# Two edits in a two-block kernel: the transposes of masked weights left out, and rotary partners moved by DMA instead of by products

## The reference

```
k_prev = jnp.concatenate([jnp.zeros_like(kb[:, :1]), kb[:, :-1]], axis=1)
kk = jnp.concatenate([k_prev, kb], axis=2)
s = jnp.einsum('bnqkgd,bnjkd->bnkgqj', qb, kk) * (HEAD_DIM ** -0.5)
mask = band[None] & ((kj >= ATTN_BLOCK)[None] | has_prev[:, None, None])
```

```
q = (rms_norm(cq, q_a_norm) @ w_qb).reshape(b, s, MLA_HEADS, MLA_QK)
q_rope = rope(q[..., MLA_NOPE:], positions)      # x1*cos - x2*sin, x1*sin + x2*cos
kv = (rms_norm(ckv, kv_a_norm) @ w_kvb).reshape(b, s, MLA_HEADS, MLA_NOPE + MLA_DV)
```

## Time and profile before

| | |
|---|---|
| device time, median of three runs | 1911.07 us |
| runs | 1910.46, 1911.07, 1912.54 us |
| span of the profiled execution (first to last instruction) | 1909.2 us |
| mean granted TensorE clock | 0.974 |
| TensorE busy | 1858.1 us (97%) |
| VectorE, ScalarE, GpSimd busy | 869.7, 774.6, 875.8 us |
| DMA, mean over the span | 91 GB/s |

### The profile page before, as it was taken

How to read it: one execution, slowest core, us unless ns; L and a number is a source line. 1 busy time by engine, 2 the same in 40 slices (tenths; PEclk the granted TensorE clock), 3 DMA queues, 4 the chain that set the end, 5 groups by cost and what they waited for, 6 DMA issues and landing times.

```text
span 1909.2 us, 25178 instructions
## 1 busy us (share of the span) xinstructions
PE 1858.1 (97%) x8910; PEld 1520.7 (80%) x8910; DVE 869.7 (46%) x1287; ACT 774.6 (41%) x1242; POOL 875.8 (46%) x1176
## 2 busy tenths in 40 slices
PE   5899999999999999999999999999999999999997
PEld 4898888888888777888888888788888878787776
DVE  8983232121126797532121126841355551466653
ACT  8753343232224477433232334423333342334662
POOL 1025455554556521655455545664445445372222
PEclk8589999999999999999999999999999999999998
DMA  4234333333323321333332333352232233231111
GB/s 162 68 99 152 96 93 104 90 99 97 101 88 99 97 72 27 111 89 99 96 102 89 99 98 90 99 150 89 88 87 79 78 89 89 62 119 56 36 53 44
DMA packets 51428, 173.59 MB, mean 91 GB/s; under 512 B 6688, under 2 KB 7072, under 8 KB 50704
## 3 DMA queue, kind: packets, MB, share of 16 engines
q1 hardware_dynamic: 49968, 169.72, 30.1%
q10 hardware_dynamic: 1376, 2.72, 0.5%
HBM read 161.21 MB, written 2.10 MB: 86 GB/s over the span
## 4 chain that ended last, share of the span: by engine, by line
PE 37%; issue 29%; POOL 27%; DVE 5%; ACT 1%; POOLq 0%; DMA 0%; ACTq 0%; SPq 0%; DVEq 0%
POOL wlo L501 27%; PE ps L997 10%; PE ps L999 10%; PE ps L998 10%; PE ps L1474 1%; PE ps L1465 1%; PE ps L1464 1%; PE ps L1220 1%; PE ps L1187 1%; DVE E L338 0%; DVE bt L334 0%; PE ps L1149 0%; DVE E L333 0%; PE ps L1399 0%; PE ps L1402 0%
## 5 line engine op out<-in xcount | busy, mean ns | idle before, releaser
L501 POOL TENSOR_TENSOR wlo<-raw,whi 128x256 fp32r<-128x256 f32 x1152 | 863.1, 781 | 984.7 <-ACT whi L548 876.1
L548 ACT ACTIVATE whi<-raw 128x1024 fp32r<-128x1024 f32 x288 | 302.0, 1052 | 369.7 <-PE ps L999 362.9
L997 PE MATMUL ps<-Ch,whi 128*128 128x512 f32 x912 | 362.7, 398 | 0.6 <-POOL wlo L501 0.6
L999 PE MATMUL ps<-Ch,wlo 128*128 128x512 f32 x912 | 355.8, 390 | 0.0
L998 PE MATMUL ps<-Cl,whi 128*128 128x512 f32 x912 | 355.5, 390 | 0.0
L997 PE MATMUL ps<-Ah,whi 128*128 128x512 f32 x640 | 255.0, 398 | 1.7 <-DVE Al L1693 1.6
L997 PE MATMUL ps<-Bh,whi 128*128 128x512 f32 x640 | 250.4, 391 | 0.0
L999 PE MATMUL ps<-Ah,wlo 128*128 128x512 f32 x640 | 249.6, 390 | 0.0
L998 PE MATMUL ps<-Al,whi 128*128 128x512 f32 x640 | 249.3, 390 | 0.0
L999 PE MATMUL ps<-Bh,wlo 128*128 128x512 f32 x640 | 249.2, 389 | 0.0
L998 PE MATMUL ps<-Bl,whi 128*128 128x512 f32 x640 | 249.1, 389 | 0.0
(11 more groups left out here) (374 smaller groups left out, 2134.9 us busy)
## 6 DMA issues: line engine op xcount, KB each, us to landing
raw<-in_w SPq DMA_DIRECT2D x288, 512.0 KB, 3.6
u<-in_xch SPq DMA_DIRECT2D x1, 2048.0 KB, 8.3
swap<-vsb SPq DMA_DIRECT2D x16, 128.0 KB, 2.3
swap<-zz SPq DMA_DIRECT2D x16, 128.0 KB, 2.3
h<-in_xfm SPq DMA_DIRECT2D x2, 1024.0 KB, 7.1
out<-h SPq DMA_DIRECT2D x8, 256.0 KB, 2.0
bB<-in_bc SPq DMA_DIRECT2D x1, 1024.0 KB, 10.3
bC<-in_bc SPq DMA_DIRECT2D x1, 1024.0 KB, 12.8
```

The costliest lines, as they stand in the source:

```text
L501: last = nc.gpsimd.tensor_tensor(wlo[:, r, cc], raw[:, r, cc], whi[:, r, cc].bitcast(F32), ALU.subtract)
L548: nc.scalar.activation(whi[:, slot, :], raw[:, slot, :], ACT.Copy).then_inc(hi_ready, 1)
L997: nc.tensor.matmul(out, whi[:, slot, w], xh, start=first, stop=False)
L999: return nc.tensor.matmul(out, wlo[:, slot, w], xh, start=False, stop=last)
```

## The change

In the grouped-query attention the transposes of an even pair start at k = 1 (PE), so that the block of weights that query block 0 has for its missing predecessor is not transposed: three instead of four for each of the two units. ACT copies only the 384 columns that were written there.

In the latent attention the four `partners` products behind the kvb strips are gone. SP moves the partners instead: `query_swap(l)` copies four pieces of 32 partitions (64 KB each) of `qr[:, l]` into `acc` (even l) or `std` (odd l), which are free by then. DVE waits for these copies (`query_in`) where it waited for the product, and reads the partner from SBUF. SP's copies stand in its order behind the loads of strips 276 (l = 0 and 1), 277 (l = 2) and 278 (l = 3), so the loop over strips is written out from 276 to 279.

```diff
+            def query_swap(l):
+
+                sp.wait_ge(evac, OUT0["kvb"] + 1)
+                if l >= 2:
+                    sp.wait_ge(rope_done, 19 + l - 1)
+                for b in (0, 64):
+                    for lo, hi in ((b, b + 32), (b + 32, b)):
+                        sp.dma_start(query_part[l % 2][lo:lo + 32, :], qr[hi:hi + 32, l, :]).then_inc(query_in[l % 2], 16)
...
+                elif t == S0["kvb"] + 1:
+                    query_swap(0)
+                    query_swap(1)
+                elif t in (S0["kvb"] + 2, S0["kvb"] + 3):
+                    query_swap(t - S0["kvb"])
...
-                    nc.scalar.copy(pt1[:, un % 2, :], ps[:, 2 + un % 2, :]).then_inc(pt_ready, 1)
+                    kept = slice(P if pair % 2 == 0 else 0, TOK)
+                    nc.scalar.copy(pt1[:, un % 2, kept], ps[:, 2 + un % 2, kept]).then_inc(pt_ready, 1)
...
-                    for k in range(4):
+                    for k in range(1 - pair % 2, 4):
                         last = nc.tensor.transpose(ps[:, 2 + un % 2, k * P:(k + 1) * P], sm1[:, un % SLOTS1, k // 2, k % 2 * P:(k % 2 + 1) * P], C("ident"))
...
                 short_strip("kvb", l, 4, 2, "L", XT["lat"], 3)
-                pe.wait_ge(evac, OUT0["kvb"])
-                if l >= 2:
-                    pe.wait_ge(rope_done, 18 + l)
-                partners(qr[:, l, :], SX + l % 2)
...
-                rotate_by(4 + l, qr[:, l, :], qr[:, l, :], ps[:, SX + l % 2, :], rcos[:, :], rsin[:, :], ev[:, 0, :], ev[:, 1, :])
+                V.tensor_tensor(ev[:, 0, :], qr[:, l, :], rcos[:, :], ALU.mult)
+                dve.wait_ge(query_in[l % 2], 64 * (l // 2 + 1))
+                ch.link(V.tensor_tensor(ev[:, 1, :], query_part[l % 2][:, :], rsin[:, :], ALU.mult))
+                V.tensor_tensor(qr[:, l, :], ev[:, 0, :], ev[:, 1, :], ALU.add).then_inc(rope_done, 1)
```

More of the change, by code:

```diff
@@ L264, in program @@
         part_in = [sem("part_in0"), sem("part_in1")]
+        query_in = [sem("query_in0"), sem("query_in1")]
         vt_ps = sem("vt_ps")
@@ L310, in program @@
         squares = (sq, cy)
+        query_part = (acc, std)
         def over(x, axis, n):
@@ L471, in _ @@
             single_strips(E0, E1)
-            with sp.Fori(E1, NS // RING) as i:
+            V0, V1 = (S0["kvb"] + 1 + LAG) // RING, (S0["kvb"] + 3 + LAG) // RING + 1
+            with sp.Fori(E1, V0) as i:
+                for r in range(RING):
+                    next_strip(i, r)
+            single_strips(V0, V1)
+            with sp.Fori(V1, NS // RING) as i:
                 for r in range(RING):
@@ L1728, in rotate_first @@
                 V.tensor_tensor(dst, part_bank, s1, ALU.add).then_inc(rope_done, 1)
[L1730 to L1734, removed]
             def feature_lows(pair):
```

## The result

The changed kernel takes 1915.46 us (median of nine runs, 1914.28 to 1917.84), against 1911.33 us for the kernel before beside it (nine runs, 1910.02 to 1912.54). The ratio is 1.0023, with a 95% interval of 1.0014 to 1.0033. So it is slower, by 4.1 us of the medians; 3.9 were predicted. The profiled execution has a span of 1912.7 us against 1909.2, 3.5 us more.

What follows compares the result with a forecast made beforehand. TensorE, busy 97% of the span, was taken to bound the kernel. Kvb's +5.4 us (pause and half clock, products gone) less 1.5 us for transposes gave 1911.07 + 3.9 = 1915.0 us; own range 1912 to 1918, 8 in 10 1909.5 to 1918.5.

Steps and rivals of the forecast that it cites:

- The transposes: Phase q: sixteen transposes left out at 0.11 us each, 1.76 us, of which 1.5 come through; bounds 0.4 and 2.0.
- The rival in which VectorE holds phase q: Phase q: TensorE's earlier arrival turns into waiting, only 0.4 us gained; +5.0 us in all, 1916.1; 15%.
- The four products: Phase kvb: four partner products gone from TensorE at 0.90 us each, 3.6 us saved if nothing replaces them.
- When the copies land: Phase kvb: first copies, issued behind strip 276's load from 1723.45, land at 1728.6; bounds 1727.7 and 1729.4.
- The rival with 4.3: Phase kvb: copies land 4.3 us after first issue, at 1727.4 to 1727.7; about 1.0 us less, 1914.0; 9%.
- What waits behind it: Phase kvb: key row 4 leaves PSUM at 1730.8, so TensorE stands still 7.0 us before the third strip.
- The rival "in time": Phase kvb: copies land before TensorE feels them, both savings stand; 5.1 us faster, 1906.0; 8%.
- The clock: Phase kvb, after TensorE's pause: half clock for some 4 us of products, losing 1.9 us; bounds 0 and 3.2.
- The rival "the clock stays up": Phase kvb: no half clock after TensorE's pause; 1.9 us less, 1913.1; 6%.
- The last copies: Scores after kvb: VectorE comes 0.8 to 1.1 us late, 1.38 us idle time absorbs it; counted as nothing.
- The rival that priced it at 1.1 us: Scores after kvb: VectorE's 1.1 us lateness isn't absorbed; +5.0 us in all, 1916.1; 12%.
- The total: Whole kernel: 5.4 - 1.5 = +3.9 us; span 1913.1 from 1909.2, median 1915.0 from 1911.07.

Runs made afterwards that it cites:

- The sixth experiment: Changed kernel with VectorE's rotation 0 put behind the second kvb strip's key rows, 1 and 2 behind the third's, 3 behind the fourth's; 1908.61 us, ratio 0.9986.
- the third: Changed kernel with each query tile's partners copied as soon as the tile is out of PSUM, into places of their own; 1906.90 us, ratio 0.9977.
- the seventh experiment: Changed kernel with the copies for l = 3 issued right behind those for l = 2, behind the load of strip 277; 1916.27 us, ratio 1.0026.
- the fourth kernel: Changed kernel with the copies of the first two query tiles moved one load forward, behind that of strip 275; 1910.25 us, ratio 0.9998.

## Why the prediction was right, step by step

The predicted 1915.0 us stands against 1915.46, and the mechanism is the one predicted. One term, the last copies, was wrong, and one argument, on the clock, rests on a misread row.

- *The transposes.* Predicted 1.76, of which 1.5 come through; measured 1.64. The step that held some back for VectorE was not needed: two pairs take 11.53 us, from 11.74, so VectorE kept up, and the wait before the last rotated query grew by 0.08 us only. The rival in which VectorE holds phase q is out.
- *The four products.* Predicted 0.90 each and 3.6 in all; measured 3.56.
- *When the copies land.* GpSimd's part was to be 0.5 us quicker; it is 3.23 instead of 3.68. The load was to follow within 0.5 us; it is 0.03. The landing was put 5.15 us behind the first copy, and is 5.46 (1721.21 to 1726.67), within the bounds. The rival with 4.3 is out. By the estimate that the prediction works out from the Trainium skill ("DMA: Bandwidth & Descriptors", section "Anatomy of one DMA — SWDGE (gpsimd) path"), which gives figures for another path, it would have been 3.95; measured on this queue, behind a 512 KB load, it is 1.5 us more.
- *What waits behind it.* Predicted a pause of 7.0 us, measured 7.3, which is the landing's difference. The sixth experiment shows that it is carried by key row 4, the third that it goes when the copies come early. The rival "in time" needed a landing 7.0 us earlier than predicted for both savings, and 3.9 us earlier to be faster than before at all; it came 0.3 us later behind the strip's end.
- *The clock.* Predicted 4 us at half clock on work, 1.9 us lost; in the changed kernel's profile 2.8 and 1.5. The other two kernels with the same pause have 5.3 and 6.05, so that the term is 1.5 to 2.9 us in these three profiled executions. It is the least certain term of the sum, and it was given such bounds. The rival "the clock stays up" is out. But the argument against it, a fall after a pause of only 2.4 us, is a misreading. These two stretches of the kernel before lie ahead of that pause, which begins at 1641.70; TensorE is busy in both, and the granted clock is 1.00 in the first and 0.50 in the second:

```profile
1640.90:1641.10 0.20, 0.20 (x4) 0.20 (x3) 0.00 (x0) 0.20 (x1) 0.00 (x0) 1.00 0.95 215
1641.20:1641.70 0.50, 0.49 (x3) 0.20 (x1) 0.00 (x0) 0.00 (x0) 0.49 (x1) 0.50 0.67 254
```

The clock was down before the pause began, so this pause can't have brought it down. That the clock fell in the 7.3 us was right; the row that was given for it didn't show it.
- *The last copies.* This step failed. VectorE was to come 0.8 to 1.1 us late to the scores and to make it up in its 1.38 us of idle time before the fourth score. It takes the first scores 1.49 us after TensorE starts them (1746.37 to 1747.86) instead of 0.75, so it is 0.7 us late, but that idle time is still there (1.37 us): TensorE's third scores wait 0.45 us for the bank of the first, which VectorE reads late, so the whole of TensorE's stream moves and with it the moment when the fourth score is ready. From the first value transpose to the fourth scores it is 9.78 us instead of 9.10. It costs 0.7 us, and the seventh experiment gives it back. The rival that priced it at 1.1 us was nearer in this point.
- *The total.* In the profiled executions kvb is +5.2 (predicted 5.4) and the last copies +0.7 (0). Phase q is -3.2 (predicted -1.5), of which 1.6 is the clock that didn't fall at 675 us, which I had not foreseen. The stretches that the change leaves alone differ by +0.8; the first of them, the same code in all nine kernels, takes 663.0 to 664.5 us in their traces. So the predicted span (1913.1) fits the profiled one (1912.7) within 0.4 us partly by luck, because terms of the other sign met. Without the clock in phase q and these stretches the terms give 5.2 + 0.7 - 1.6 = +4.3 us, and the medians +4.1, where 5.4 + 0 - 1.5 = 3.9 was predicted; here too the last copies' 0.7 us is partly hidden by the two other terms. The medians of single edits are coarser: each edit against a kernel without it gives -1.5 and -3.3 us for the transposes, and +5.8 and +7.6 us for the copies, each known to about 2 us.

## What to carry to other kernels

When an instruction of the bounding engine is replaced by a DMA, look for the moment at which the copy is issued and for what stands in its queue's order before it. A copy that is free in itself costs its whole lateness, when the instruction that waits for it has something queued behind it that the bounding engine needs. Issue it where its source becomes ready (here 1906.90 in place of 1915.46 us), or let the waiting engine do first what others want (1908.61). Idle time of an engine further on makes up a delay only if the bounding engine isn't held in between by what the late engine has yet to read.

## What the runs showed of the hardware

- Four copies of 64 KB from SBUF to SBUF behind a 512 KB load on the same queue landed 5.46 us after the first issue (in the five other kernels where VectorE waited for them, 5.19 to 5.50). SyncE issues one in 0.6 us (four in 2.42).
- The clock's fall isn't a matter of the pause's length alone. In the long pause of the changed kernel it fell 3.4 us after TensorE stopped. After 1.8 us (the fourth kernel) it fell 1.5 us after work had begun again, after 1.2 us (the sixth) it stayed up, and after 1.9 to 2.0 us in phase q it fell, 0.4 to 0.8 us after work had begun again, in three traces and stayed up in six.
- After pauses of nearly the same length (7.15, 6.97, 7.18 us) it stayed down on 2.8, 5.3 and 6.05 us of work. Filling such a pause with products that nobody reads kept it up, and the work behind it took 1.4 us less.
